# A two-layer decoder trunk: two passes of a hardware loop against one unrolled program

## The reference

```python
h = rms_norm(x, attn_norm)
z = h @ w_in                      # 1024 x 3104: the inputs of three head groups
a = gated_delta_rule(...)         # 4 heads x 64: short conv, decay, chunks of 64, gated norm
b = nsa_attention(...)            # 8 heads x 64: compressed, selected and window branches
c = B * conv3(C * X)              # 256 channels
x = x + concat(a, b, c) @ w_out
h = rms_norm(x, ffn_norm)
x = x + (silu(h @ w_gate) * (h @ w_up)) @ w_down
```

## Time and profile before

| | |
|---|---|
| time, median of 3 runs | 1681.86 us (1677.52 to 1689.7) |
| span of the profiled execution | 1687.8 us, 21379 instructions |
| PE busy (weight loads) | 1532.4 us, 91% (1281.8 us, 76%) |
| DVE busy | 764.4 us, 45% |
| POOL busy | 567.0 us, 34% |
| ACT busy | 543.1 us, 32% |
| DMA: share of 16 engines, bytes | 23.4%, 114.87 MB |
| code and tables loaded by DMA ("instruction" queue q8) | 70 packets, 1.15 MB |

### The profile page before, as it was taken

One profiled execution on the slowest core, in us unless ns is written; L12 is line 12 of the kernel. 1 busy time (PEld: TensorE's weight loads), 2 busy tenths in 40 slices (PEclk: granted clock), 3 DMA queues, 4 the chain that ended last, 5 costly groups with the idle time before them and its releaser, 6 DMA issues. The chain is left out here.

```text
span 1687.8 us, 21379 instructions
## 1 busy us (share of the span) xinstructions
PE 1532.4 (91%) x8570; PEld 1281.8 (76%) x8570; DVE 764.4 (45%) x1468; ACT 543.1 (32%) x925; POOL 567.0 (34%) x251
## 2 busy tenths in 40 slices
PE   5789886999989999999977899879998999999995
PEld 4678885666978888888766788756678888888884
DVE  5755557666143320332256554586743333123322
ACT  4342223554132221222234322155542322122211
POOL 4263231111324444444332641320303444444441
PEclk9998997998999999999988889979999999999998
DMA  6213200000123323332231141100002233233322
GB/s 156 78 51 76 69 26 25 26 1 1 51 75 100 100 88 100 100 100 94 69 83 53 51 94 50 50 25 2 1 1 75 75 100 94 94 100 100 100 87 100
DMA packets 184515, 114.87 MB, mean 68 GB/s; under 512 B 46176, under 2 KB 172128, under 8 KB 184416
## 3 DMA queue, kind: packets, MB, share of 16 engines
q1 hardware_dynamic: 184416, 113.48, 23.4%
HBM read 110.58 MB, written 2.88 MB: 67 GB/s over the span
## 5 line engine op out<-in xcount | busy, mean ns | idle before, releaser
L1097 POOL TENSOR_TENSOR w_lo<-w_raw,w_hi 128x2048 fp32r<-128x2048 f32 (+1 forms) x100 | 453.0, 4530 | 726.1 <-ACT w_hi L864 726.1
L864 ACT ACTIVATE w_hi<-w_raw 128x2048 fp32r<-128x2048 f32 (+1 forms) x100 | 188.7, 1887 | 591.1 <-PE ps L461 591.0
L461 PE MATMUL ps<-hT_hi,w_lo 128*128 128x512 f32 x928 | 233.4, 394 | 0.0
L461 PE MATMUL ps<-hT_hi,w_hi 128*128 128x512 f32 x896 | 226.7, 396 | 0.0
L461 PE MATMUL ps<-hT_lo,w_hi 128*128 128x512 f32 x896 | 223.9, 392 | 0.0
L461 PEld LDWEIGHTS ps<-hT_hi,w_lo 128*128 128x128 f32 x928 | 176.4, 191 | 36.6
L461 PEld LDWEIGHTS ps<-hT_lo,w_hi 128*128 128x128 f32 x896 | 169.0, 189 | 35.6 <-issue 0.3
L461 PEld LDWEIGHTS ps<-hT_hi,w_hi 128*128 128x128 f32 x896 | 169.1, 190 | 35.0 <-issue 0.3
L873 ACT ACTIVATE arena<-ps 128x512 f32<-128x512 f32 (+5 forms) x268 | 124.7, 477 | 173.1 <-PE ps L572 88.9
L1616 DVE TENSOR_TENSOR ffn_tmp<-ps,ffn_tmp 128x512 f32<-128x512 f32 x44 | 30.4, 691 | 296.2 <-ACT ffn_tmp L1078 296.2
L1562 DVE TENSOR_TENSOR aT_lo<-ffn_tmp,aT_hi 128x512 fp32r<-128x512 f32 x44 | 143.8, 3268 | 30.7 <-ACT aT_hi L873 30.7
(11 more groups left out here) (262 smaller groups left out, 1886.6 us busy)
## 6 DMA issues: line engine op xcount, KB each, us to landing
w_raw<-in_w_gate_up SPq DMA_DIRECT2D x88, 512.0 KB, 5.0
w_raw<-in_w_in SPq DMA_DIRECT2D x22, 1024.0 KB, 5.4
w_raw<-in_w_down SPq DMA_DIRECT2D x16, 1024.0 KB, 5.0
w_raw<-in_w_out SPq DMA_DIRECT2D x8, 1024.0 KB, 5.2
w_raw<-in_w_down SPq DMA_DIRECT2D x8, 768.0 KB, 4.5
w_raw<-in_w_in SPq DMA_DIRECT2D x2, 1120.0 KB, 5.4
w_raw<-in_w_in SPq DMA_DIRECT2D x2, 1056.0 KB, 7.5
x_tok<-in_x SPq DMA_DIRECT2D x4, 512.0 KB, 5.3
```

What stands on the lines that cost most here:

```text
L461: mm = nc.tensor.matmul(out_ap, a(ab, k), b(bb, k), start=first and i == 0, stop=last and i == len(kts) - 1)
L864: nc.scalar.activation(whi[:, c % 2, 0:kt * w], raw[:, c % 2, 0:kt * w], ACT.Copy).then_inc(S["w_hi"], 1)
L1097: nc.gpsimd.tensor_tensor(wlo[:, c % 2, 0:kt * w], raw[:, c % 2, 0:kt * w], whi[:, c % 2, 0:kt * w].bitcast(F32), ALU.subtract).then_inc(S ...
```

## The change

The two layers stand in one program: the loop over layers is done in the Python code that writes the instructions, in one block, without loop, branches, barriers and clearing of semaphores. Semaphores count on through both layers; `S.at(name, value, layer)` adds what a layer adds to a counter (a table), so each wait keeps its meaning.

- **Parameters.** Each layer has its own parameter tiles. Layer 1's are loaded in the setup, behind x and weight tiles 0 and 1; layer 2's in the middle of layer 1, on SP behind the load of weight tile 16. `cw` has a semaphore of its own, and the wait for the other parameters moves to where they are used.
- **Norm at the boundary.** PE transposes the token tiles one by one as the norm delivers them, first blocks 4 to 7 of each tile, then blocks 0 to 3; ACT, DVE and `first_group` follow in this order, and the first product goes to bank 4.
- **Weight tile 0 of the next layer** is copied and subtracted at the end of the layer before, by ACT ahead of the squares.
- **The end.** The last layer makes no norm and loads no next weight tiles; each token tile of x is stored by a DMA of 512 KB behind its last add.

The code is written anew with `l` as an argument, and each wait reads `S.at(...)`. The core of the diff, without the waits that only change their form:

```diff
+        def at(self, name, value, layer):
+            return self[name], layer * PER_LAYER.get(name, 0) + value
...
+    def in_bank(n):
+        return 4 if n == 0 else n % IN_BANKS
...
+        prm = [Params(sb(f"an{l}", [P, KD]), sb(f"fn{l}", [P, KD]), sb(f"cw{l}", [P, 6, 4]), ...
+               for l in range(DEPTH)]
...
+        def load_params(sp, l):
+            p = prm[l]
+            for dst, src in ((p.an[:], ...), (p.fn[:], ...)):
+                sp.dma_start(dst, src).then_inc(S["norm_gains"], 16)
...
+            params = [(p.cw[:, j], A["gdn_conv_w"][l]...[j]) for j in range(6)]
+            params += [(p.w2c[:], ...), (p.scw[:, 0], ...), (p.scw[:, 1], ...), (p.alog[:], ...), ...]
+            params += [(p.pe_c[:, k], ...) for k in range(2)]
+            for i, (dst, src) in enumerate(params):
+                sp.dma_start(dst, src).then_inc(S["conv_w" if i < 6 else "params"], 16)
...
-        def clear():
-            nc.all_engine_barrier()
-            ids = sorted(s.num for s in S.values())
-            nc.gpsimd.sem_clear(range(ids[0], ids[-1] + 1))
-            nc.all_engine_barrier()
-        clear()
...
+        def norm_order(tag):
+            return [0, 1, 2, 3, 4, 5, 6, 7] if tag == "1" else [4, 5, 6, 7, 0, 1, 2, 3]
...
-        with nc.Fori(0, DEPTH) as l:
-            with nc.Block() as block:
...
+        def sync_layer(sp, l):
             for c in range(2, N_CHUNKS):
...
+                if c == FFN0 and l + 1 < DEPTH:
+                    load_params(sp, l + 1)
+            if l + 1 < DEPTH:
                 for c in range(2):
...
+        def sync_finish(sp):
+            for t in range(NT):
+                sp.wait_ge(*S.at("x_down", 12 + t + 1, DEPTH - 1))
+                sp.dma_start(out[0, t * P:(t + 1) * P, :], x[:, t, :]).then_inc(S["stored"], 16)
+            sp.wait_ge(S["stored"], 16 * NT)
...
             def norm_transposes(tag):
+                order = norm_order(tag)
                 for t in range(NT):
+                    if tag == "1":
+                        pe.wait_ge(*S.at("hn1", t + 1, l))
+                    elif l == 0:
+                        pe.wait_ge(S["consts"], 1)
+                        pe.wait_ge(S["hn_first"], t + 1)
+                    else:
+                        pe.wait_ge(*S.at("hn_next", t + 1, l - 1))
+                    for k in order[:4]:
                         mm = block(k, t)
+                mm.then_inc(S["hps" + tag], 4)
+                if tag == "1":
+                    pe.wait_ge(*S.at("x_res", 16, l))
+                elif l:
+                    pe.wait_ge(*S.at("x_down", 16, l - 1))
+                for k in order[4:]:
...
             def split_hi(c, l=l):
                 if c >= N_CHUNKS:
+                    c, l = c - N_CHUNKS, l + 1
+                if l == DEPTH:
                     return
                 if c < 2:
+                    act.wait_ge(S[f"prefetched{c}"], 16 * (l + 1))
+                    if l:
+                        act.wait_ge(*S.at("mm", mm_count(N_CHUNKS - 2 + c), l - 1))
...
+            if l == 0:
                 split_hi(0)
...
+                    if c + 2 <= N_CHUNKS:
+                        split_hi(c + 2)
+            if l + 1 < DEPTH:
                 for t in range(NT):
+                    act.wait_ge(*S.at("x_down", 12 + t + 1, l))
+                    norm_square(act, t, "ssq_next", l)
...
-                    dve.wait_ge(S["params"], 16 * N_PARAMS)
-                    chain(V.tensor_scalar(cw[:], cw[:], 0.5, None, ALU.mult))
+            dve.wait_ge(*S.at("conv_w", 96, l))
+            chain(V.tensor_scalar(prm[l].cw[:], prm[l].cw[:], 0.5, None, ALU.mult))
...
-                                if f == 1 and ch == 1 and t:
+                        if l + 1 < DEPTH and f == 1 and ch == 1 and t:
...
-                sp.dma_start(out[0].rearrange("(t p) d -> p t d", p=P), x[:]).then_inc(S["stored"], 16)
```

More of the change, by code:

```diff
@@ L18 @@
+from collections import namedtuple
 from contextlib import ExitStack
@@ L242, in norm_scale @@
             for t in range(t0, t1):
-                nc.vector.tensor_scalar(hn[:, t, :], x[:, t, :], y[:, t - t0:t - t0 + 1], None, ALU.mult).then_inc(done, 1)
-        with nc.Block() as block:
[L247 to L313, removed]
@@ L325, in mm_count, with scalar_setup @@
+        def scalar_setup(act):
+            for t in range(NT):
+                act.wait_ge(S[f"x_in{t}"], 16)
+                norm_square(act, t, "ssq_first", 0)
+            act.wait_ge(S["angles"], 1)
+            nc.scalar.activation(cossin[:], cossin[:], ACT.Sin).then_inc(S["rope"], 1)
+            act.wait_ge(S["rope"], 1)
         def mm_count(c):
@@ new lines, in scalar_layer @@
+                if last:
+                    split_hi(c + 2)
+                if e == "act":
+                    empty_group(n)
+                if n >= HOP_GROUP and slots < 7 * NT:
+                    hop_act(slots)
+                    slots += 1
+                if n == 20:
+                    act.wait_ge(*S.at("cmp_u", 1, l))
+                    nc.scalar.activation(hid[:, 2, :], hid[:, 1, :], ACT.Tanh, scale=0.7978845608028654
+                                         ).then_inc(S["cmp_th"], 1)
@@ new lines, in scalar_layer @@
+                if n == 12:
+                    for i in range(2):
+                        act.wait_ge(*S.at("gback", 5 + i, l))
+                        ev(qdT[:, i, :], ps[:, 7 if i == 0 else 3, :]).then_inc(S["gT"], 1)
+                if 13 <= n <= 16:
+                    t = n - 13
+                    act.wait_ge(*S.at("dec", t + 1, l))
+                    nc.scalar.activation(dA, dA, ACT.Exp, scale=-1.0)
+                    nc.scalar.activation(dB, dB, ACT.Exp).then_inc(S["dexp"], 1)
@@ new lines, in scalar_layer, with exp @@
+            for h in range(NH):
+                act.wait_ge(*S.at("qps", h // 2 + 1, l))
+                rows = slice(h % 2 * HEAD, (h % 2 + 1) * HEAD)
+                ev(qst[rows, h, :], ps[rows, Q_BANKS[h // 2], :]).then_inc(S["qhi"], 1)
+            def exp(s):
+                i = s % NT
+                act.wait_ge(*S.at("nmax", s + 1, l))
+                if s >= 5:
+                    act.wait_ge(*S.at("ptr", s - 4, l))
+                n = (i + 1) * P
+                nc.scalar.activation(prob[s % 5][:, 0:n], ps[:, i, 0:n], ACT.Exp, bias=att[:, 0, s % 8:s % 8 + 1],
+                                     accum_out=att[:, 1, s % 8:s % 8 + 1]).then_inc(S["exp"], 1)
```

2417 lines of the change are left out of this document (1227 added, 1190 removed).

## The result

The change takes 1672.53 us (median of 9 runs, 1667.86 to 1673.49) against 1681.86 before; the ratio is 0.9944, 95% interval [0.9932, 0.9956]. 9.3 us are won where 18.2 were forecast.

A forecast was written before the change was run, and what follows sets the result against it. TensorE (PE), busy 91% of the span, was taken as the bound, so only its idle time could be won: tail 13.8 + hand-over 4.4 + start 0 = 18.2 us, from 1681.9 to 1663.7 us, 80% range 1654 to 1672.

The forecast's parts named there:

- Tail: End of the last layer: residual adds without norms, then a smaller last store; 13.8 us won (10.0 to 14.9).
- the store: Last store at the program's end: 512 KB taking 2.8 us instead of 2048 KB taking 6.6.
- Hand-over and `cw`: Between layers: norm tile to `hT_hi` 7.44 to 1.22 us, POOL costs 1.4, earlier `cw` wins 0.9; 4.4 won with table loss.
- Start: Program start: fourth norm tile waits for POOL, `hT_hi` 1.2 us later, `cw` gives 0.9 back; about zero (-1.2 to +4.5).
- rival 1: At the start the fourth norm tile slips past POOL, `hT_hi` 3.4 us earlier; 1659.4 us; chance 22%.
- Table: Activation table load falls amid layer 2's gates, where PE waits: 1.28 us lost; in layer 1 zero.
- rival 2: The clock gives it back: layer 2 runs like layer 1, 6.2 us longer; 1669.9 us; chance 13%.
- Parameters: zero: Layer 2's 18 parameter DMAs, behind weight tile 16 in layer 1, are covered by a pause of PE and ACT: zero.
- Rival 3: At the end the last store costs as much as the big one, 6.6 us instead of 2.8; 1667.5 us; chance 9%.
- rival 4: Unrolled code fetched late, misses like the loop jump's 3.9 us on PE; 1683.2 (five) or 1698.8 (nine); chance 4%.

The follow-up runs named there:

- the old distances: The changed kernel with layer 2's parameter tiles placed behind the large scratch area, so aT_hi and aT_lo stand at their former distance from w_hi: 1664.72 us, ratio to before 0.9893.
- the larger set of runs of before: The unchanged kernel before, measured beside its repeat run: 1682.26 us (25 runs, one of them above 1685).
- the loop at the new addresses: The kernel before, with loop, barriers and tail, but on-chip tensors from x to the scratch area at the change's addresses: 1680.05 us, ratio 0.9990.
- the first profile: The profile of the unchanged kernel read for the prediction: span 1687.8 us, one of its longest executions, against a median of 1681.86 us.

## Why the prediction was wrong

*Tail*: right. 13.8 forecast (10.0 to 14.9); 12.7 measured for norm and store and 1.8 read for `clear()` and the branch, 14.5 in all; of this the store 3.8 forecast and 4.1 measured.

*Hand-over and `cw`*: right. 6.2 won by 7.44 becoming 1.27, 1.4 lost to POOL (1.53 instead of 0.16), 0.9 for `cw` (0.94). Alone, with its table load and with the 1.8 us at the end taken off, it is worth 3.1 to 8.1, forecast 4.4.

*Start*: right, near zero; the fourth norm tile waits for POOL, and rival 1 did not come.

*Table*: here it failed. "1.28 lost" is what the load costs PE where it stands (1.41 more of waiting). At the change's addresses it costs 6.6 in the time (1672.53 to 1665.89). Priced as a wait alone, it left out that layer 2 then runs through another sequence of clock levels: what it loses at the gates is made up by 272 us into the layer, and some 6 us go in the attention behind. That is rival 2: it spoke of 6.2 and 1669.9, from a layer 2 of 455.9 instead of 449.7, and 454.7 came. It was given 13%, because nothing said what would set it off; and its long layer came from one of the longest executions of the kernel before. The result lies 0.5 above the 1672 at which the range ended.

*Parameters: zero* failed too. It priced the DMAs and missed an edit: layer 2's parameter tiles, 2176 bytes in each partition, and a smaller reserve of on-chip memory (`dynamic_dma_scratch_size=2048`, which the core of the diff doesn't show) move every tensor behind them. By the paces that is 4.6 lost and 3.4 won, 1.2 in all; no run shows these 1.2 us in the time. But the old distances alone, with the late load left in, win 7.8. So the 6 us or so of the long layer belong to load and addresses together; booking them under the table, as here, is a choice.

With the measured terms: 14.5 + 4.8 + 0.9 - 6.6 - 1.2 = 12.4 won, against 9.3 (9.7 against the larger set of runs of before; the interval is 7.4 to 11.4). Where the other 3 us went is not shown; the terms come from different runs and have errors of their own. Rival 3 did not come (2.6, not 6.6), nor rival 4: where PE waits over 2.5 us after (16 places, at most 6.65), it does so at the places of before, but for the norms' transposes and the gates; none is like the jump's.

What stays open: the late load alone doesn't make the long layer. All nine profiles with the late load and `w_down` at 232 ns or more have it (453 to 456 us); the three with the late load and less than 230 don't (450.7, 451.8, 450.7), nor do those without a late load at either pace. Each of these is one execution, and the gap between the two kinds is 1.3 us; but all nine have the clock at 1.2 GHz for 13.7 us where, 357 to 368 us behind `hT_hi`, the short ones have 3.4 (only layer 2 of the loop at the new addresses has 17.1). (Layer 1 of the first profile was long in the same place with neither, the only such layer.) Some executions of the same kernels took 1661.51 and 1668.34 us where most take 1672 and 1679; no profile is of one of these. Taking away either one is shown to be enough; why it needs both, and what carries the difference from the gates to the attention 200 us later, is not shown.

## What to carry to other kernels

Here one late load, which made PE wait 1.4 us longer, cost 6.6 at one set of addresses and not at another, by the clock far behind it. So a wait in such a place has two prices; price the second with the clock's stretches of the same kernel, and take the chance of that case from how often they differ between like layers. When tiles are added, compare the addresses of everything behind them. When an edit puts an old part back to measure its worth, compare its rows with the old ones: here 1.8 us of the old tail stayed away. And look at which tables are loaded where once a loop is gone: one tiny operation in an idle place moved the load and won 6.6 us.

## What was not expected of the hardware

The pace of back-to-back fp32r products depended on where their operands start. `w_hi` starts at remainder 128 of 256 bytes; with `aT_hi` at remainder 64, 128, 192 and 0 the 512-column products came every 229.2, 226.7, 233.9 and 232.4 ns, and the 256-column ones every 117.8, 119.9, 113.4 and 118.7. What in the chip does this is not shown, nor whether it is the remainder or the distance to `w_hi` that counts: `w_hi` was never moved against the 256 bytes, and no remainder was tried at two distances. Delays of 0.7 and 1.5 us on the path at the hand-over don't show in the time (1672.8 and 1672.42 against 1672.53), while 2.96 and 6.20 cost 3.6 and 6.2.
